# An encoder kernel on one core: TensorE multiplies ones until the memory arrives, memory rows are scaled one by one, query weights are split behind the x tiles they meet, and the first output rows are split during the memory attention

## What is computed

```python
def trunk(x, mem, p):
    for i in range(2):
        h = rmsnorm(x, p['norm_in'][i])
        z = h @ w_in[i]                      # queries, keys, values, q_mem, gate
        mix = mla_mixer(...) if i == 0 else swa_mixer(...)
        mem_o = memory_attention(q_mem, mem, p['mem_norm'][i], p['w_mem_kv'][i], ...)
        branch = concatenate([mix, mem_o]) * silu(gate)
        x = x + branch @ p['w_out'][i]

def memory_attention(q, mem, mem_norm, w_mem_kv, q_norm, k_norm):
    q = rmsnorm(q per head, q_norm)
    kv = rmsnorm(mem, mem_norm) @ w_mem_kv   # 1024 x 1024: keys, then values
    k = rmsnorm(kv keys per head, k_norm)
    return softmax(q k^T * 128**-0.5) v      # 4 heads of 128
```

## Time and profile before

| | |
|---|---|
| median of 3 runs | 1371.09 us (1370.33 to 1372.25) |
| profiled execution | 1369.96 us, its span 1368.2 us |
| TensorE busy | 1342.0 us of the span (98%) |
| TensorE idle | 26.2 us |
| VectorE, ScalarE, GpSimd busy | 889.4, 679.2, 402.4 us (65%, 50%, 29%) |
| transfers | 248.20 MB, mean 181 GB/s |

### The profile page before, as it was taken

One profiled execution on the slowest core, in us unless ns is written; L12 is line 12 of the kernel. 1 busy time (PEld: TensorE's weight loads), 2 busy tenths in 40 slices (PEclk: granted clock), 3 DMA queues, 4 the chain that ended last, 5 costly groups with the idle time before them and its releaser, 6 DMA issues.

```text
span 1368.2 us, 20477 instructions
## 1 busy us (share of the span) xinstructions
PE 1342.0 (98%) x7160; PEld 1163.7 (85%) x7160; DVE 889.4 (65%) x1792; ACT 679.2 (50%) x1547; POOL 402.4 (29%) x517
## 2 busy tenths in 40 slices
PE   6999999999999999999999999999999999999999
PEld 5789987888888889888888899888888888898887
DVE  7765588887795656888674433667776634266871
ACT  6444466555464546787552422555454323157660
POOL 1131243321002323756302212413300112337560
PEclk9999999999999999999999999999999999999999
DMA  6865774343768487634776446522144652654225
GB/s 238 291 231 182 247 259 167 123 164 112 270 220 289 153 274 251 229 123 137 271 256 224 138 134 192 182 89 84 60 166 141 197 173 88 219 174 155 97 74 185
DMA packets 109334, 248.20 MB, mean 181 GB/s; under 512 B 11056, under 2 KB 48816, under 8 KB 109232
## 3 DMA queue, kind: packets, MB, share of 16 engines
q1 hardware_dynamic: 103760, 239.19, 51.3%
q10 hardware_dynamic: 5472, 7.69, 1.8%
HBM read 158.76 MB, written 88.08 MB: 180 GB/s over the span
## 4 chain that ended last, share of the span: by engine, by line
PE 85%; DVE 7%; ACT 4%; DMA 2%; issue 1%; POOL 1%; SPq 0%; ACTq 0%; DVEq 0%; POOLq 0%
PE bank L1839 24%; PE bank L1841 24%; PE bank L1840 24%; PE bank L1884 7%; PE bank L1845 2%; PE bank L2190 2%; PE bank L1846 2%; ACT prob L772 2%; DVE w_split L1134 1%; DVE probT L1141 1%; POOL rr L1662 1%; DVE part_split L1134 1%; DVE prob L1584 1%; ACT w_split L739 1%; ACT o_low L1076 0%
## 5 line engine op out<-in xcount | busy, mean ns | idle before, releaser
L1839 PE MATMUL bank<-actT,w_split 128*128 128x512 f32 x544 | 214.9, 395 | 0.0
L1841 PE MATMUL bank<-actT,w_split 128*128 128x512 f32 x544 | 212.3, 390 | 0.0
L1134 DVE TENSOR_TENSOR w_split<-w_raw,w_split 128x512 fp32r<-128x512 f32 (+3 forms) x212 | 150.5, 726 | 89.6 <-ACT w_split L739 84.5
L1718 POOL TENSOR_TENSOR prob<-prob,rinv 128x256 f32<-128x256 f32 x192 | 132.1, 719 | 251.7 <-DVE rinv L1265 251.7
L739 ACT ACTIVATE w_split<-w_raw 128x512 fp32r<-128x512 f32 (+3 forms) x212 | 126.2, 607 | 128.7 <-PE bank L1841 53.9
L1839 PE MATMUL bank<-w_split,actT 128*128 128x512 f32 (+3 forms) x512 | 171.1, 334 | 1.8 <-DVE actT L1344 1.2
L1840 PE MATMUL bank<-w_split,actT 128*128 128x512 f32 (+3 forms) x512 | 170.2, 332 | 0.0
L1841 PE MATMUL bank<-w_split,actT 128*128 128x512 f32 (+3 forms) x512 | 170.2, 332 | 0.0
L1840 PE MATMUL bank<-actT,w_split 128*128 128x512 f32 x384 | 149.9, 390 | 0.0
L754 ACT ACTIVATE sq<-bank 128x512 f32<-128x512 f32 (+4 forms) x128 | 60.4, 480 | 132.8 <-PE bank L1841 125.8
L1141 DVE TENSOR_TENSOR probT<-bank,probT 128x512 fp32r<-128x512 f32 (+1 forms) x192 | 111.8, 638 | 20.8 <-ACT probT L745 19.1
(11 more groups left out here) (181 smaller groups left out, 3118.9 us busy)
## 6 DMA issues: line engine op xcount, KB each, us to landing
kept_w<-w_split SPq DMA_DIRECT2D x112, 512.0 KB, 4.9
w_split<-kept_w SPq DMA_DIRECT2D x112, 512.0 KB, 3.9
w_raw<-in_w_mem SPq DMA_DIRECT2D x64, 256.0 KB, 3.6
w_raw<-in_w_out SPq DMA_DIRECT2D x48, 256.0 KB, 3.9
kept_w<-part_split SPq DMA_DIRECT2D x24, 512.0 KB, 4.2
w_raw<-in_w_b SPq DMA_DIRECT2D x48, 256.0 KB, 3.8
part_split<-kept_w SPq DMA_DIRECT2D x24, 512.0 KB, 4.1
w_raw<-in_w_a SPq DMA_DIRECT2D x32, 256.0 KB, 3.7
```

Of the source, the lines that this page charges most:

```text
L1134: dve.tensor_tensor(halves(n)[1], w_raw[:, RAW_AT[n] % RAW, 0:width], halves(n)[0].bitcast(fp32), ALU.subtract).then_inc(w_lo_dve, 1)
L1718: pool.tensor_tensor(t, t, rinv[:, par, i:i + 1].to_broadcast(list(t.shape)), ALU.mult).then_inc(p_pool, 1)
L1839: nc.tensor.matmul(out, lhs[0], rhs[0], start=start, stop=False, skip_group_check=skip)
L1841: return nc.tensor.matmul(out, lhs[1], rhs[0], start=False, stop=stop, skip_group_check=skip)
```

## The change

It has four parts, and one order that follows from them.

1. TensorE multiplies ones by ones: 11 matmuls of 128x512 once two memsets are done (one of them new on DVE, over actT's first tile), and 2 more when the first small tables have landed. They write to a bank that nothing reads. ACT waits for the last of them before it writes actT.
2. GpSimd computes the scale of each memory block as soon as that block's squares are summed, and DVE scales it; DVE splits one weight tile behind each block, and the fourth only behind the first two pairs of memT. The eps for the memory keys is computed after both.
3. In L = 0 the splits of memV's tiles 4 to 7 are spread over the squares and sums of x (`FIRST_WEIGHTS`), x_scales comes after the sixth key tile in place of the fifth, and x tile 3 is loaded one weight tile earlier. In all layers the splits of qmem's tiles come behind the x tile that they meet (`X_WEIGHTS`), none ahead of the first.
4. The four tiles of part 0 of L = 0 and 2 stand in the list among the gate tiles of the memory attention, one after every second gate tile, and are split (L = 0) or reloaded (L = 2) there.

```diff
+FIRST_WEIGHTS = (1, 1, 2, 2, 3, 4, 4, 4)
+X_WEIGHTS = (1, 2, 3, 4, 4, 4, 5, 6)
+PART_IN = ("gates", "late")
...
-                if phase == "late" and names[0][0] == "gate" and k % 4 == 3:
-                    part_rows(L, 0, [names[0][2] - 4 + k // 4])
+                if phase == PART_IN[l] and names[0][0] == "gate" and k % 4 == 3:
+                    part_rows(L, 0, [names[0][2] % 4 + k // 4])
...
-                if p + 1 < len(PARTS[0]):
+                if 0 < p + 1 < len(PARTS[0]):
                     part_rows(L, p + 1)
...
-                    return chunks["part", L, p, 1, 1][-1] + (0 if p == 0 and step == 0 else 1)
+                    return chunks["part", L, p, 1, 1][-1] + 1
...   SP
-                load_weights(RAW + 1, RAW + 4)
+                load_weights(RAW + 1, RAW + 3)
                 load_x(0, 3)
-                load_weights(RAW + 4, FIRST["qmem", 0, NT - 1])
+                load_weights(RAW + 3, FIRST["qmem", 0, NT - 1])
...   ACT
+                        w_hi_to(v_at + SPLIT + 1)
                         for f in range(KD):
                             x_square(L, f)
-                            if f == 3:
-                                w_hi_to(v_at + SPLIT + 1)
-                            elif f == 5:
-                                w_hi_to(v_at + SPLIT + 4)
+                            w_hi_to(v_at + SPLIT + FIRST_WEIGHTS[f])
...
                     w_hi_to(k_at + X_SCALE_AT + 4)
-                    w_hi_to(q_at + 1)
+                    if L == 0:
+                        act.wait_ge(warm_done, 1)
                     for k in range(KD):
...
-                        w_hi_to(q_at + min(k + 2, SPLIT + max(0, k - 3) // 2))
+                        w_hi_to(q_at + X_WEIGHTS[k])
...   ACT and DVE, first pair
-                                w_hi_to(CHUNKS["aQ", L, p + 1, NT - 1][-1] + (3 if p == 0 else 1))
+                                w_hi_to(CHUNKS["aQ", L, p + 1, NT - 1][-1] + 1)
...   DVE
-                    dve.wait_ge(rrm_ready, 1)
                     for i in range(NM):
+                        dve.wait_ge(rrm_ready, i + 1)
                         count("xn")
                         dve.tensor_scalar(xn[i], mem_in[:, i, :], rr_m[:, i:i + 1], None, ALU.mult).then_inc(xn_ready, 1)
-                    w_lo_to(FIRST["memV", 0, NM - 1] + SPLIT)
+                        w_lo_to(FIRST["memV", 0, NM - 1] + i + 1)
                     for j in range(KD // 2):
+                        w_lo_to(FIRST["memV", 0, NM - 1] + (SPLIT if j > 1 else SPLIT - 1))
...
+                dve.memset(actT[:, 0, :].bitcast(fp32), 1.0).then_inc(warm_set, 1)
...
-                            if f == 4:
-                                w_lo_to(v_at + SPLIT + 1)
-                            elif f == 6:
-                                w_lo_to(v_at + SPLIT + 4)
+                            w_lo_to(v_at + SPLIT + FIRST_WEIGHTS[f - 1])
                             x_add(L, f)
...
                     norm_lo(x_slots[:, 0, :])
-                    w_lo_to(q_at + 1)
+                    w_lo_to(k_at + X_SCALE_AT + 4)
                     dve.wait_ge(*full(("xR", L)))
                     x_scaled_tile(L, 0)
                     for k in range(KD):
...
-                        w_lo_to(q_at + min(k + 1, SPLIT + max(0, k - 3) // 2))
                         dve.wait_ge(hi_done, count("hi"))
...
-                        w_lo_to(q_at + min(k + 2, SPLIT + max(0, k - 3) // 2))
+                        w_lo_to(q_at + X_WEIGHTS[k])
...   GpSimd
-                        memory_scales(0)
+                        for j in range(NM):
+                            pool.wait_ge(ssm_ready, j + 1)
+                            rsqrt(ss_m[:, j:j + 1], rr_m[:, j:j + 1], 1, D, rrm_ready)
+                        link(pool.tensor_scalar(eps_m[:, 0:NM], ss_m[:, 0:NM], EPS / D, EPS * EPS, ALU.mult, ALU.add))
...   TensorE
+                def warm(n):
+                    for _ in range(n):
+                        ins = nc.tensor.matmul(psum[BANKS - 1][:], ones[:], actT[:, 0, :], start=True, stop=True)
+                    return ins
+
+                pe.wait_ge(ones_set, 1)
+                pe.wait_ge(warm_set, 1)
+                warm(11)
                 pe.wait_ge(first_in, 32)
-                pe.wait_ge(ones_set, 1)
+                warm(2).then_inc(warm_done, 1)
...
-                    mem_chunk("memK", {X_SCALE_AT: x_scales} if L > 0 else {0: x_sums, 4: x_scales})
+                    mem_chunk("memK", {X_SCALE_AT: x_scales} if L > 0 else {0: x_sums, 5: x_scales})
```

More of the change, by code:

```diff
@@ L517, in trunk_kernel @@
             ones_set = sem("ones_set")
+            warm_set = sem("warm_set")
+            warm_done = sem("warm_done")
             max_ready = sem("max_ready")
@@ L872, in _ @@
                         if L > 0 and j == 0:
-                            act.wait_ge(rrm_ready, G + 1)
+                            act.wait_ge(rrm_ready, NM + G)
                         hi(use, v0[:, 0, 2 * j:2 * j + 2, :], bank(use)[:].rearrange("p (a b) -> p a b", a=2),
@@ L1508, in _ @@
                             if more:
-                                w_lo_to(CHUNKS["aQ", L, p + 1, NT - 1][-1] + (3 if p == 0 else 1))
+                                w_lo_to(CHUNKS["aQ", L, p + 1, NT - 1][-1] + 1)
                             else:
```

## The result

The changed kernel takes 1363.31 us (median of 4 runs, 1362.15 to 1364.05) against 1370.92 us (4 runs, 1370.33 to 1372.25): ratio 0.9941, 95% interval 0.993 to 0.9953. That is faster by 7.6 us. The forecast was 5.1 us and its range ended at 1363.6: the direction was right and the gain 2.5 us larger than the sum. The profiled execution took 1364.05 us, 5.9 less than the profiled one of before, with a span of 1362.2.

What follows compares the result with a forecast made beforehand. TensorE was taken to bound the kernel, its idle time lying in the first 45 us and 180 to 225 us. 3.5 + 0.2 + 1.6 - 0.2 = 5.1 us off 1371.09 gave 1366.0, range 1363.6 to 1368.9.

Steps and rivals of the forecast that it cites:

- The ones: Matmuls of ones in TensorE's idle time before the first memory block: gain 0 for the transposes and 0 for memV.
- The moved part rows: Four splits and 4 loads and stores moved into L = 0's memory attention: cost 0.2 us, bounds 0 and 2.8.
- No wait left in the first pair: Sign at the first pair of heads: no wait at lines 1884 and 1839 once part tiles are moved.
- The gate tiles: Rival in the memory attention: gate tiles come late, TensorE waits 3.2 us at four places, 1378.6 us; chance 0.04.
- memV at 12.1: memV's first matmul starts at 12.1 instead of 14.05, ACT's high halves coming last: gain 1.95 us.
- The part tiles: First pair of heads, 180 to 225 us: three TensorE waits for DVE go, gain 1.6 us, bounds 0 and 2.0.
- L = 1: qmem in L = 1 to 3: TensorE does not wait at its start, so the new order gives 0.
- The start: Up to qmem in L = 0: qmem starts at 35.45 instead of 38.95, gain 3.5 us, bounds 2.1 and 4.05.
- the weight last: Ahead of qmem: its first tile's load, issued at 29.4, takes 4.54 us; low half done by 35.3, qmem at 35.45.
- The x work: Ahead of qmem: x_scales behind 84 matmuls, full at 32.0; 2.15 us of x work end at 34.2, before the weight.
- Inside qmem: TensorE's wait of 0.37 us at 55.73 in qmem of L = 0: gain 0.2 us, bounds 0 and 0.37.
- The clock rival: TensorE's clock falls before memV after sparse transposes, costing 0.7 to 1.25 us: about 1367.1 us; chance 0.12.

Runs made afterwards that it cites:

- again: The changed kernel unaltered, run again: 1362.68 us against 1370.04 for the kernel before, ratio 0.9944.
- no_ones: The changed kernel without the matmuls of ones, their memset and the wait for them: 1363.27 us, ratio 0.9948 to the kernel before.
- x_only: The kernel before with only the new order of qmem's splits (`X_WEIGHTS`), in all four layers: 1367.82 us against 1371.12, ratio 0.9971.
- old_order_later: The changed kernel with the old order of qmem's splits in L = 1 to 3: 1365.27 us against 1370.74 for the kernel before, ratio 0.996.
- start_only: The changed kernel with part 4 of the change taken back: 1366.97 us against 1371.12 for the kernel before, ratio 0.9964.
- part_only: The kernel before with only part 4 of the change (part 0's tiles among the gate tiles): 1368.38 us against 1370.04, ratio 0.9987.
- rows_only: The kernel before with only the memory blocks scaled one by one: 1369.71 us against 1371.12, ratio 0.9989.
- again2: The changed kernel unaltered, a third time: 1363.77 us, ratio 0.995 to the kernel before.
- the bridge: The changed kernel with 3 and 5 more matmuls of ones behind the transposes of memory blocks 0 and 1: 1363.8 us, ratio 0.995.
- no_ones2: The changed kernel without the ones, a second time for its profile: one run, 1364.64 us.

## Where the prediction held, and the steps that failed

**Right.** The ones worth nothing to the measured time (*again* against *no_ones*, 0.6 us apart, where the runs of each spread over 3.6 us or more). The moved part rows hidden in the memory attention, at 0 instead of the 0.2 that the sum charged. No wait left in the first pair. The gate tiles not late. memV at 12.1 was right in its number and lucky in it: in the first trace GpSimd's factor of block 1 came 0.4 us later than worked out and ACT's queue ended 0.3 us sooner, so that the bank came last.

**The part tiles, 1.6 forecast, 2.4 to 2.5 measured,** above the upper bound of 2.0. The mechanism was right and its size was off. The sum added the idle times 0.57 + 0.28 + 0.78 = 1.63. Between the starts of the matmuls on both sides of these waits lie 0.73 + 0.53 + 0.95 = 2.21 us more than between the same matmuls of the changed kernel, and the steps just behind the first and the third wait are 0.15 and 0.13 us longer: 2.49 in all. The ends of matmuls overlap, so a wait costs what the distance between starts grows by, not the idle time that is printed. The row at 416.30 shows the same on one wait: 0.38 idle, but 0.76 from start to start, 0.53 above the pitch of 0.23, and the matmul behind it starts 0.34 later where the pitch is 0.23, another 0.11.

**L = 1, 0 forecast, 0.8 to 1.0 measured.** This is a step that failed as a mechanism, and not only in size: "In L = 1 to 3 TensorE does not wait at the start of qmem, so the order there costs and gives 0". At the start it doesn't; in the midst of qmem, at 416.30, it did. *x_only* gains 0.8 there with the new order alone, and *old_order_later* loses the gain with the old order alone. The trace of before held the row, and the prediction looked at the start only. *start_only* gains 0.78 there; *part_only*, *rows_only* and *old_order_later*, which keep the old order, lose 0.13 to 0.18. In L = 2 and 3 nothing can be put down to the order: between 854 and 1070 us the shift grows by 0.73 or 0.74 in eleven traces of the fifteen laid beside that of before, those of *part_only* and *rows_only* among them, so this step belongs to the one trace of before (it waits there for a memory weight at 1067.43, by 0.28). *again* goes back from -7.95 behind L = 1 to -6.71 at the end. About 1.0 of it falls in L = 2 between 695 and 714 and between 843 and 854 us, where TensorE waits for a split memory weight (0.25, at 697.65) and for a reloaded tile (0.17, at 844.86). Waits of this kind, up to 0.8 us, stand in other traces with the new order and with the old, at other tiles; what makes them differ is left open.

**The start, 3.5 forecast: 2.1 in the first trace, 3.66 and 4.08 in two others of the same kernel.** Three things each set qmem's start in some execution. If the clock falls before memV, x_sums come 1.55 us later behind memV's start, and so does all behind them. With the clock up, the x chain ends it, at 34.87 to 35.5. If the transfer of the weight takes 5.45 to 6.32 us instead of 4.54, the weight ends it, at 35.8 to 36.7. The forecast had the weight last, at 4.54, a duration that it took from one trace and that ran from 3.3 to 6.3 in others. Here too the path was not the one worked out. The x work was to end at 34.2 and did so in *again*, but by luck: x_scales stand behind 86 matmuls and not 84 (x_sums' two were left out, 0.46 us), and memV began 0.45 us sooner than forecast. In *again2*, with memV at 12.07 as forecast, the x work ends at 34.63. And the weight's low half stands behind it and not ahead of it, which adds 0.66 us to the start. VectorE's timeline in *again*:

```profile
33.46 0.75 DVE L1349 SCALAR_TENSOR_TENSOR actT<-q_st,gcol,actT 128x512 fp32r<-128x512 f32 x1 [0.25 <-ACT actT L894]
34.13 0.69 DVE L1141 TENSOR_TENSOR w_split<-w_raw,w_split 128x512 fp32r<-128x512 f32 x1
```

**Inside qmem** 0.45 for 0.2: the wait of 0.37 between starts went wholly, and the stretched step behind it with it.

**The sum.** With the terms as measured when the clock is up, 3.7 to 4.1 + 0.45 + 2.4 + 0.8 = 7.4 to 7.8 us; the medians of the changed kernel give 7.6, 7.4 and 7.2 in three sets. The sum of 5.1 was short by L = 1, by the waits priced at their idle time, by the 0.2 charged for the moved rows, and by up to 0.6 at the start. The profiled execution happened to be one with the lower clock and shows 5.9, against an execution of before that was itself 1.0 us below its median.

**The clock rival** came true in the trace and hardly in the medians. Over all profiles with the new start: with the change's ones memV began at the lower clock in 3 of 6 (the first, *start_only*, *old_order_later*), with the bridge in 0 of 4, without ones at half pitch in 2 of 3 (*rows_only*, *no_ones2*; there it had not fallen, since the transposes before it took 0.24 each, but not yet risen). With the old start it was 0 of 3 (before, *part_only*, *x_only*). The mean clock recorded for each run agrees, though it doesn't tell where in the run the clock was low: with the change's ones it reads 0.998 or 0.999 in 11 of 29 runs, with the bridge in 0 of 16, in the kernels with the old start in 5 of 65, and 1.000 in the rest. In each of the five sets with the change's ones that have both kinds of run, those with the lower mean are slower, by 0.5 to 1.8 us, 1.2 on average; the rival had put 0.7 to 1.25 on it. So the fall costs about that where it comes, the bridge keeps the clock up, and the medians hardly show it. The Trainium skill, "TensorE: Matmul & The Clock Gate", Part 1, says that an idle stretch closes the gate again; the traces agree as far as that it fell only behind the sparse 5 us. The Trainium skill, same page, Part 4, says that transposes do not count as activity in the same way. The fall behind 16 transposes fits that; the three old starts, where memV followed transposes alone at full pitch, speak against it. These counts are small, and why one execution falls and the next doesn't stays open.

## What to carry to other kernels

A wait costs the growth of the distance between two starts. In the waits measured here that was 0.16 to 0.25 us more than the idle time printed, and the steps just behind took up to 0.15 more: sum distances. When an order changes in a loop over all layers, look through every layer for the waits of that form, and not only at the place for which the order was made. Where several chains end within a us of each other (here clock, x work and a transfer), one trace names the one that was last in that execution; profile the kernel twice or more before correcting any of them, and when a forecast time comes out, check in the chain that the forecast link set it.

## What the hardware showed that I had not expected

The granted clock fell to 0.50 for 3.4 us right behind 13 matmuls and 16 quick transposes, and in other executions of the same program it did not. The column of the clock can read 1.00 at the start of a trace while the matmuls run at half pitch: four per us in *no_ones2* and *rows_only*, against six in *again*. The same load of 256 KB took 3.3 to 6.3 us from issue to landing behind the same five small tables, and 2.6 to 2.7 us ahead of them.
